# Gated tiles turned between projections, attention's inputs read by 256 tokens with the bias in two parts, memory low parts on two engines

## The chip, the cores and the metric

One core of one Trainium2 chip. The time is the device time of one launch in microseconds. Engines are named as in the profile: PE (TensorE matmuls), PEld (its weight loads), DVE (VectorE), ACT (ScalarE), POOL (GpSimd), SP (SyncE, which only issues transfers here).

## The reference, cut to what matters

Sequence and width are 1024. `@` products are held in float32 quality. Cut to the parts that the change touches:

```
h = layer_norm(x)
proj = h @ w_in                                   # 1024 x 2560
z_a, q_b, k_b, v_b = split(proj)                  # 1024, 512, 512, 512 columns
u, v = split(gelu(z_a)); v = layer_norm(v)        # 512 columns each
s = w_sp(masked, 4 groups of 128x128) @ v + b_sp  # within blocks of 128 tokens
y_a = u * s
# attention: 8 heads of 64; a chunk of 64 queries sees its chunk and 8 before it
scores = q_b k_b^T / 8 + rel_bias[clip(distance, -128, 128)]
y_b = softmax(scores) @ v_b
h = layer_norm(a*h + [y_a, y_b] @ w_out)
k, v = mem @ w_xk, mem @ w_xv                     # memory: 256 x 1024
h = layer_norm(a*h + cross_attention(h @ w_xq, k, v) @ w_xo)
h = layer_norm(a*h + peer(h))                     # expert retrieval, untouched
```

## The kernel before, in words

Every float32 operand of a product is split in two fp32r parts, a high one (ACT, `Copy`) and a low one (raw minus high, on DVE or POOL), and `three` (L106 to L108) issues three matmuls per product. The stages run one after the other, with a barrier and freed semaphores (`free_sems`) between them. Each stage is written out per engine; an engine runs its instructions in order and waits on semaphores. The input of a product is held turned (features on the partitions) in `aT_hi` and `aT_lo`, in an early half (tokens 0 to 511) and a late half.

**Projection** (`project_stage("pin", ..., gated=True)`). 40 units: 5 blocks of 512 columns by 8. Blocks 0 and 1 (units 0 to 15) give u and v through a gelu on ACT; blocks 2 and 3 (16 to 31) give q and k turned; block 4 (32 to 39) gives v_b. A unit is 24 matmuls of 512 columns on PE, one copy out of PSUM (ACT for gelu, DVE at L620 else) and one store by SP (L565). In block 4 unit 32 + i reads token tile i of `aT`. While a block runs, the four weight pieces of the next are loaded by SP at even units (L549), their high parts are made by ACT (L584), the low parts of pieces 0 and 2 by POOL (L574), those of 1 and 3 by DVE (L608, at units 2 and 6 of a block).

**Gating** (`class Gating`) rides on these units. `tile(u, delay)` says which of the 8 token tiles has a step at unit u: tile j loads at unit 16 + 3j (L410, L413), is normalised by DVE at 17 + 3j (`vector_step`, L444 to L453), and is mixed by PE at 19 + 3j (12 matmuls of 128 columns before the unit's own), with y = (s + b) u on DVE (L461) in the same step. With EVERY = 3 tile 7 is mixed at step 40, behind the last unit. Then `finish_tensor`, `finish_scalar` and `finish_vector` turn the eight y tiles: 4 transposes on PE (L496), a high part (L502) and a low part (L507) each, over two PSUM banks, into the first four feature groups of `aT`.

**Attention** (`attention_stage`). 64 units: 8 query tiles of 128 tokens by 8 heads. Tile n looks at nk = 128, 256, 384, 512 keys for n = 0 to 3 and at 640 from n = 4 on. Per unit PE makes scores (three or six matmuls), DVE adds the bias and takes the maximum (L789) and its negative (L793), ACT takes the exponential (L761), DVE the reciprocal (L800) and the product (L802), PE turns the probabilities (L839), ACT and DVE split them (L755, L808), PE multiplies by v. Step u has the scores and softmax of unit u, the product of u - 1, the turning of u - 2 and the values of u - 3; the outputs of a pair of heads are split every second step (L769, L813). The inputs come back from HBM in 12 pieces of 512 KB through a raw buffer of two places: q and k by 128 features of all 1024 tokens (rows of 4 KB), in turn for the four pairs of heads, then v by 256 tokens. SP waits for a piece's low part before it loads the next but one. Pieces 2u + 2 and 2u + 3 are split in step u (ACT L744; DVE L775 for q and k, POOL L738 for v), behind the softmax of unit u. The bias, 640 columns of 8 heads spread over 128 partitions (2,560 KB), is one transfer behind the first two pieces (L726); POOL masks two corners of it (L733, L734), and DVE's first L789 waits for both.

**Memory** (`memory_stage`). Four blocks of 512 columns of `w_xk` and `w_xv`, each in four weight pieces over four raw places: SP loads (L901) when the low part of the piece four before is made, ACT makes the high part (L924), POOL every low part (L908). PE runs 4 units of 24 matmuls of 256 columns for each block of w_xk, and 2 of 24 of 512 columns for each of w_xv.

Behind this come the projection of w_xq, cross attention, a norm stage, the key scores and the expert stages, which take the rest of the span from about 660 us on.

Of the kernel before, what the change touches and what calls it, by code (L numbers as in the profile page):

```python
# [57 lines left out]
def layer_program(nc, x, mem, ln_in_g, ln_in_b, w_in, gate_ln_g, gate_ln_b, w_sp, b_sp, rel_bias, w_out,  # L58
# [51 lines left out]
    with top:  # L110
# [247 lines left out]
        class Gating:  # L358
# [3 lines left out]
            FIRST, EVERY, SETUP = 16, 3, 8  # L362
# [127 lines left out]
            def finish_tensor(self, pe):  # L490
                for j in range(TT):
# [7 lines left out]
            def finish_scalar(self, act):  # L499
                for j in range(TT):  # L500
# [3 lines left out]
            def finish_vector(self, dve):  # L504
                for j in range(TT):
# [4 lines left out]
        def project_stage(tag, weight, blocks, gated=False):  # L510
# [21 lines left out]
            with ExitStack() as stage:  # L532
# [7 lines left out]
                after = range(len(units), len(units) + 3)  # L540
                with nc.Block() as block:
# [36 lines left out]
                    def _(act):  # L578
# [9 lines left out]
                        for u, (b, i) in enumerate(units):  # L588
# [7 lines left out]
                            if gated:  # L596
                                gate.scalar_step(act, u)
                        if gated:
                            for u in after:
                                gate.scalar_step(act, u)  # L600
                            gate.finish_scalar(act)

                    @block.vector
                    def _(dve):
# [8 lines left out]
                        for u, (b, i) in enumerate(units):  # L613
# [7 lines left out]
                            if gated:  # L621
                                gate.vector_step(dve, u)
                        if gated:
                            for u in after:
                                gate.vector_step(dve, u)
                            gate.finish_vector(dve)

                    @block.tensor
                    def _(pe):
                        for u, (b, i) in enumerate(units):  # L630
                            if gated:
                                gate.tensor_step(pe, u)
                            if u >= BANKS:
# [14 lines left out]
                        if gated:  # L648
                            for u in after:
                                gate.tensor_step(pe, u)  # L650
                            gate.finish_tensor(pe)


        def attention_stage():


            bias_in, masked = sem("at_bias_in"), sem("at_masked")
            raw_in = [sem(f"at_raw_in{i}") for i in range(2)]
# [21 lines left out]
            with ExitStack() as stage:  # L680
# [12 lines left out]

                pieces = []
# [19 lines left out]
                with nc.Block() as block:  # L714
                    @block.sync
                    def _(sp):
                        for n, (src, _, _) in enumerate(pieces):

                            if n >= QK + 2:
                                sp.wait_ge(sp_lo_v, n - QK - 1)  # L720
                            elif n >= 2:
                                sp.wait_ge(sp_lo, n - 1)
                            sp.dma_start(raw_of(n), src).then_inc(raw_in[n % 2], 16)
                            if n == 1:

                                sp.dma_start(bias[:], bass.AP(ext_d.tensor, ext_d.offset,  # L726
                                                              [[1, P], [EXT, B_HEADS], [1, SPAN]])).then_inc(bias_in, 16)

                    @block.gpsimd
                    def _(pool):  # L730

                        pool.wait_ge(bias_in, 16)
# [3 lines left out]
                        for n in range(QK, len(pieces)):  # L736
# [1402 lines left out]
```

## Time and profile before

| | us |
|---|---|
| median of 3 runs | 3589.03 (3585.22 to 3593.11) |
| the profiled execution, its own time | 3612.53 |
| its span | 3610.7 |
| PE busy | 3108.0 (86%) |
| DVE busy | 2120.6 (59%) |
| POOL busy | 1449.8 (40%) |
| mean granted clock | 0.931 |

The span is that of one profiled execution, whose own time stands 23.5 us above the median of the runs; durations below are from it. A stretch gives its length, then for PE, PEld, DVE, ACT and POOL the busy time with the number of instructions, then PEclk, the busy share of the DMA engines and their GB/s. PEclk is the granted TensorE clock as a share of 2.4 GHz (0.50 is the lower level, 1.2 GHz). In a timeline each row gives start, length, engine, line, operation, tile written and tiles read, and in brackets the idle time before it and what ended it; "x8" are merged instructions. A matmul's length holds its way through the pipeline; the distance of two starts is what it costs.

### The profile page before, as it was taken

How to read it: one execution, taken by the hardware profiler on the slowest of the kernel's cores; microseconds unless marked ns; L12 is line 12 of the kernel's file. 1: busy time of each engine (PE TensorE's matmuls, PEld its weight loads, DVE VectorE, ACT ScalarE, POOL GpSimd, SP SyncE). 2: the span in 40 equal slices, each digit the busy share in tenths (PEclk: the TensorE clock that was granted, in tenths of full speed). 3: DMA queues.
4: the chain of work that ended last, by engine and by line, in shares of the span. 5: the costliest groups of instructions: out<-in, count | busy, mean ns of one | idle time of the engine just before them, and what ended most of it. 6: DMA issues, size and time to landing. Idle time of an engine off the chain costs nothing. (4 is left out here: it accounts for less than half of the span.)

```text
span 3610.7 us, 42790 instructions
## 1 busy us (share of the span) xinstructions
PE 3108.0 (86%) x16184; PEld 2408.3 (67%) x16184; DVE 2120.6 (59%) x4483; ACT 1191.5 (33%) x1931; POOL 1449.8 (40%) x1116
## 2 busy tenths in 40 slices
PE   4995989788879979999999989766659989899997
PEld 3874777677668858888777766544436666676665
DVE  4143784215332267888877686666557667664447
ACT  3212452314221124444333333678712222222222
POOL 3100002410210025555776667667735444524542
PEclk9997599899989989999999999988879999999998
DMA  4333003321323178888999999899999999999993
GB/s 157 105 100 131 1 5 136 117 85 56 130 81 81 49 249 305 329 321 339 391 410 379 410 387 412 309 408 383 393 363 362 351 361 363 353 331 358 389 368 125
DMA packets 368045, 937.45 MB, mean 260 GB/s; under 512 B 31440, under 2 KB 130264, under 8 KB 366816
## 3 DMA queue, kind: packets, MB, share of 16 engines
q0 software_dynamic: 147456, 536.94, 38.8%
q1 hardware_dynamic: 220384, 397.77, 31.0%
q8 instruction: 130, 2.13, 0.2%
q14 instruction: 75, 0.61, 0.0%
HBM read 827.60 MB, written 106.98 MB: 259 GB/s over the span
## 5 line engine op out<-in xcount | busy, mean ns | idle before, releaser
L1419 POOL DMA_INDIRECT ex_ring<-in_expert_v,ex_idxT_sb x400 | 452.6, 1131 | 420.9 <-PE ex_ps_v L1444 217.3
L1419 POOL DMA_INDIRECT ex_ring<-in_expert_u,ex_idx_sb x328 | 407.6, 1243 | 398.7 <-DVE ex_hg L1428 230.6
L1428 DVE CUSTOM_DVE_ANT_0 ex_ring<-ex_ring,ex_xg 128x1024 f32<-128x1024 f32 x328 | 392.7, 1220 | 105.9 <-DMA ex_ring<-in_expert_u,ex_idx_sb 62.7
L106 PE MATMUL eo_ps<-eo_v_hi_sb,aT_late_hi 128*128 128x512 f32 x1024 | 413.2, 404 | 36.6 <-DVE aT_late_lo L2016 36.6
L106 PE MATMUL ex_ps_h<-aT_late_hi,ex_uT_hi_sb 128*128 128x512 f32 x1024 | 414.3, 405 | 34.8 <-issue 17.1
L107 PE MATMUL eo_ps<-eo_v_lo_sb,aT_late_hi 128*128 128x512 f32 x1024 | 404.7, 395 | 0.0
L108 PE MATMUL ex_ps_h<-aT_late_hi,ex_uT_lo_sb 128*128 128x512 f32 x1024 | 403.4, 394 | 0.0
L108 PE MATMUL eo_ps<-eo_v_hi_sb,aT_late_lo 128*128 128x512 f32 x1024 | 402.5, 393 | 0.0
L107 PE MATMUL ex_ps_h<-aT_late_lo,ex_uT_hi_sb 128*128 128x512 f32 x1024 | 401.6, 392 | 0.0
L1444 PE MATMUL ex_ps_v<-ex_ring,ex_w_sb 128*32 128x512 f32 x1600 | 252.8, 669 | 123.8 <-DMA ex_ring<-in_expert_v,ex_idxT_sb 94.3
L2024 DVE TENSOR_TENSOR eo_acc<-eo_acc,eo_ps 128x1024 f32<-128x1024 f32 x124 | 151.3, 1220 | 299.0 <-PE eo_ps L108 222.3
L106 PEld LDWEIGHTS eo_ps<-eo_v_hi_sb,aT_late_hi 128*128 128x128 f32 x1024 | 195.4, 191 | 138.3 <-issue 59.6
L1980 ACT ACTIVATE eo_v_hi_sb<-eo_v_raw 128x1024 fp32r<-128x1024 f32 x124 | 131.3, 1059 | 437.0 <-DMA eo_v_raw<-in_expert_v 336.7
L106 PEld LDWEIGHTS ex_ps_h<-aT_late_hi,ex_uT_hi_sb 128*128 128x128 f32 x1024 | 194.0, 189 | 108.9 <-issue 57.9
L1419 POOL DMA_INDIRECT ex_ring_more<-in_expert_u,ex_idx_sb x161 | 214.8, 1334 | 103.3 <-issue 41.5
L1560 ACT ACTIVATE ex_uT_lo_sb<-ex_ps_t 128x1024 fp32r<-128x1024 f32 x128 | 131.7, 1029 | 376.3 <-PE ex_ps_t L1743 248.9
L1428 DVE CUSTOM_DVE_ANT_0 ex_ring_more<-ex_ring_more,ex_xg 128x1024 f32<-128x1024 f32 x161 | 192.0, 1220 | 57.0 <-DMA ex_ring_more<-in_expert_u,ex_idx_sb 45.7
L108 PEld LDWEIGHTS eo_ps<-eo_v_hi_sb,aT_late_lo 128*128 128x128 f32 x1024 | 195.4, 191 | 42.6
L108 PEld LDWEIGHTS ex_ps_h<-aT_late_hi,ex_uT_lo_sb 128*128 128x128 f32 x1024 | 193.9, 189 | 43.0
L107 PEld LDWEIGHTS eo_ps<-eo_v_lo_sb,aT_late_hi 128*128 128x128 f32 x1024 | 195.7, 191 | 38.8
L107 PEld LDWEIGHTS ex_ps_h<-aT_late_lo,ex_uT_hi_sb 128*128 128x128 f32 x1024 | 194.4, 190 | 36.9
L1444 PEld LDWEIGHTS ex_ps_v<-ex_ring,ex_w_sb 128*32 128x32 f32 x1600 | 53.5, 116 | 234.8 <-issue 234.0
(332 smaller groups left out, 6629.4 us busy)
## 6 DMA issues: line engine op xcount, KB each, us to landing
ex_u_raw<-in_expert_u SPq DMA_DIRECT2D x128, 512.0 KB
eo_v_raw<-in_expert_v SPq DMA_DIRECT2D x124, 512.0 KB
act_d<-ex_act SPq DMA_DIRECT2D x128, 256.0 KB
gate_d<-ex_gate SPq DMA_DIRECT2D x8, 4096.0 KB
eo_g_raw<-gate_d SPq DMA_DIRECT2D x64, 512.0 KB
eo_a_raw<-act_d SPq DMA_DIRECT2D x124, 256.0 KB
h_d<-n_row SPq DMA_DIRECT2D x24, 512.0 KB, 2.6
pin_raw<-in_w_in SPq DMA_DIRECT2D x20, 512.0 KB
```

The costliest lines, as they stand in the source:

```text
L106: pe.matmul(ps, l_hi, r_hi, start=first, stop=False)
L107: pe.matmul(ps, l_hi, r_lo, start=False, stop=False)
L108: return pe.matmul(ps, l_lo, r_hi, start=False, stop=last)
L1419: pool.indirect_dma_start(rows(n), None, table, bass.IndirectOffsetOnAxis(at, 0)).then_inc(ring_in[slot[n]], 16)
L1428: dve.tensor_tensor_reduce(out=u, in0=u, in1=xg[:, j, :], scale=1.0, scalar=0.0, op0=ALU.mult, op1=ALU.add, accum_out=hg[:, j, k:k + 1]).t ...
L1444: last = pe.matmul(ps_v[32 * q:32 * q + 32, col], spreads[:, q, 31 * i + 31:31 * i + 63], rows(at[q])[:, col], start=i == 0, stop=i == 31)
L1560: act.activation(uT_lo[:, e % 2, :, :], ps_t[e % 2][:].rearrange("p (k t) -> p k t", t=P), ACT.Copy).then_inc(uT_lo_done, 1)
L1980: act.activation(v_hi[:, b, x, :], v_raw(e), ACT.Copy).then_inc(v_hi_done, 1)
L2024: dve.tensor_tensor(acc[:, t, :], acc[:, t, :], ps[t % 2][:], ALU.add).then_inc(added[t % 2], 1)
```

## The change

In gating EVERY becomes 2, so that tile j loads at unit 16 + 2j, is normalised at 17 + 2j and mixed at 19 + 2j (tile 7 at unit 33), and tile j is turned at step 34 + j: six of them before units 34 to 39, two behind the last. In attention q, k and v are read by 256 tokens (q and k with rows of 1 KB over all four feature groups), all q and k pieces without a wait, since their raw data lies in the room of the v parts of the same tokens; the bias is read in a near part (128 columns of each head, rows of 512 bytes) and a far part (512 columns). The pieces of tokens 256 and up are split in named later steps (`SPLIT_AT`), and the first low and high parts needed are those of tile pair 0 alone. The first softmax waits for the near mask, that of tile 1 for the far one. In the memory stage DVE makes every odd low part.

```diff
-            FIRST, EVERY, SETUP = 16, 3, 8
+            FIRST, EVERY, SETUP, TURN = 16, 2, 8, 34
...
-            def finish_tensor(self, pe):
-                for j in range(TT):
+            def turned(self, u):
+                return u - self.TURN if 0 <= u - self.TURN < TT else None
+
+            def turn_tensor(self, pe, u):
+                j = self.turned(u)
+                if j is not None:
                     pe.wait_ge(self.y_done, A_GROUPS * (j + 1))
                     if j >= 2:
                         pe.wait_ge(self.lo_done, j - 1)
...
-                after = range(len(units), len(units) + 3)
+                after = range(len(units), Gating.TURN + TT)
...
                             if gated:
                                 gate.scalar_step(act, u)
+                                gate.turn_scalar(act, u)
                         if gated:
                             for u in after:
-                                gate.scalar_step(act, u)
-                            gate.finish_scalar(act)
+                                gate.turn_scalar(act, u)
...
                             if gated:
                                 gate.vector_step(dve, u)
+                                gate.turn_vector(dve, u)
...
                             if gated:
                                 gate.tensor_step(pe, u)
+                                gate.turn_tensor(pe, u)
                             if u >= BANKS:
                                 out_of_psum(pe, u - BANKS)
...
-                for f in range(QF):
-                    pieces.append((qb_d[f * P:(f + 1) * P, :], q_hi[:, f, :], q_lo[:, f, :]))
-                    pieces.append((kb_d[f * P:(f + 1) * P, :], k_hi[:, f, :], k_lo[:, f, :]))
                 for f in range(TT // 2):
-                    pieces.append((vb_d[2 * f * P:2 * (f + 1) * P, :].rearrange("(a p) n -> p a n", p=P),
+                    tok = slice(f * W, (f + 1) * W)
+                    for d, hi, lo in ((qb_d, q_hi, q_lo), (kb_d, k_hi, k_lo)):
+                        pieces.append((d[:, tok].rearrange("(f p) t -> p f t", p=P), hi[:, :, tok], lo[:, :, tok]))
+                    pieces.append((vb_d[f * W:(f + 1) * W, :].rearrange("(a p) n -> p a n", p=P),
                                    v_hi[:, 2 * f:2 * f + 2, :], v_lo[:, 2 * f:2 * f + 2, :]))
-                QK = 2 * QF
+                SPLIT_AT = {0: (2,), 2: (3,), 3: (4,), 5: (5,), 10: (6,), 11: (7,), 13: (8,), 18: (9,), 19: (10,), 21: (11,)}
 
                 def raw_of(n):
-                    r = raw[:, n % 2, :]
-                    return r if n < QK else r.rearrange("p (a n) -> p a n", a=2)
+                    f, part = divmod(n, 3)
+                    if part == 2:
+                        return raw[:, f % 2, :].rearrange("p (a n) -> p a n", a=2)
+                    return (v_hi, v_lo)[part][:, 2 * f:2 * f + 2, :].rearrange("p a n -> p (a n)").bitcast(F32).rearrange("p (f t) -> p f t", f=QF)
...
+                        load(0)
+                        load(1)
+                        sp.dma_start(bias[:, :, 0:P], spread_bias(0, P)).then_inc(near_in, 16)
+                        for n in range(2, 6):
+                            load(n)
+                        sp.dma_start(bias[:, :, P:SPAN], spread_bias(P, SPAN)).then_inc(far_in, 16)
+                        for n in (6, 7, 9, 10):
+                            load(n)
+                        for f in range(2, TT // 2):
+                            sp.wait_ge(sp_lo_v, f - 1)
+                            load(3 * f + 2)
...
+                        pool.wait_ge(near_in, 16)
                         pool.memset(bias[0:CHUNK, :, 0:CHUNK], MASKED).then_inc(masked, 1)
+                        pool.wait_ge(masked, 1)
+                        split_v(0)
+                        pool.wait_ge(far_in, 16)
+                        pool.wait_ge(sp_lo_v, 1)
                         pool.memset(bias[CHUNK:P, :, SPAN - CHUNK:SPAN], MASKED).then_inc(masked, 1)
...
-                            for n in range(2 * u + 2, min(2 * u + 4, len(pieces))):
+                            for n in SPLIT_AT.get(u, ()):
                                 split(n)
...
-                            if n == 0 and hd % 2 == 0:
-                                pe.wait_ge(sp_lo, 2 * (hd // 2) + 2)
+                            if n % 2 == 0 and hd == 0:
+                                pe.wait_ge(sp_lo, n + 2)
...
-                                sp.wait_ge(lo_done, n - 3)
+                                sp.wait_ge(lo_done[n % 2], n // 2 - 1)
...
-                        for n in range(4 * PIECES):
+                        for n in range(0, 4 * PIECES, 2):
...
-                        for u in range(len(units)):
+                        n = 1
+                        for u, (b, i) in enumerate(units):
+                            while n < min(4 * PIECES, (b + 2) * PIECES):
+                                nb, q = divmod(n, PIECES)
+                                dve.wait_ge(hi_done, n + 1)
+                                dve.tensor_tensor(w_lo[:, nb % 2, 2 * q:2 * q + 2, :], raw[:, n % 4, :, :],
+                                                  w_hi[:, nb % 2, 2 * q:2 * q + 2, :], ALU.subtract).then_inc(lo_done[1], 1)
+                                n += 2
                             dve.wait_ge(out_hi, u + 1)
```

## Rows read from the trace of the kernel before

**Rows 1.** The page: granted clock in 40 slices of 90.27 us, in tenths

```profile
PEclk9997599899989989999999999988879999999998
```

**Rows 2.** Stretches of attention (first six) and of the memory stage: length, engines, PEclk, DMA

```profile
319.20:332.10 12.90, 0.91 (x6) 0.72 (x6) 2.46 (x3) 3.40 (x3) 1.04 (x2) 0.50 0.93 357
332.10:367.50 35.40, 10.40 (x42) 8.18 (x42) 15.98 (x54) 16.13 (x36) 9.35 (x4) 0.50 0.37 122
367.50:384.90 17.40, 16.63 (x78) 13.64 (x79) 12.90 (x57) 8.92 (x33) 0.00 (x0) 0.50 0.00 1
384.90:408.30 23.40, 23.40 (x110) 18.65 (x111) 15.85 (x57) 10.27 (x32) 0.00 (x0) 0.50 0.00 1
408.30:436.50 28.20, 28.20 (x145) 21.97 (x146) 18.50 (x57) 12.07 (x32) 0.00 (x0) 0.55 0.00 1
436.50:532.00 95.50, 84.72 (x821) 75.73 (x822) 84.30 (x226) 56.88 (x128) 0.00 (x0) 1.00 0.01 1
658.00:726.00 68.00, 53.24 (x304) 48.05 (x304) 8.43 (x14) 22.84 (x30) 37.71 (x16) 0.84 0.43 139
```

**Rows 3.** Waits of PE, 60 to 330 us: total, times, longest

```profile
PE ga_ps_s L106 <- DVE ga_v_lo L453: 4.6, 8, 2.4
```

**Rows 4.** Timeline of PE, projection: start, length, what, idle before it

```profile
229.31 0.39 PE L108 MATMUL pin_ps<-aT_late_hi,pin_wlo 128*128 128x512 f32 x1
...
232.05 0.33 PE L106 MATMUL ga_ps_s<-ga_v_hi,ga_wT_hi 128*128 128x128 f32 x1 [2.35 <-DVE ga_v_lo L453]
...
234.37 0.73 PE L106 MATMUL pin_ps<-aT_early_hi,pin_whi 128*128 128x512 f32 x1
...
242.16 0.39 PE L106 MATMUL pin_ps<-aT_late_hi,pin_whi 128*128 128x512 f32 x1
...
252.81 0.39 PE L108 MATMUL pin_ps<-aT_early_hi,pin_wlo 128*128 128x512 f32 x1
...
254.80 0.45 PE L106 MATMUL pin_ps<-aT_late_hi,pin_whi 128*128 128x512 f32 x1
```

**Rows 5.** Timeline of all engines, end of projection to the first softmax

```profile
307.72 0.68 DVE L620 TENSOR_SCALAR pin_res<-pin_ps 128x512 f32<-128x512 f32 x1
...
309.25 1.06 PE L496 MATMUL ga_ps_y<-ident,ga_y_sb 128*128 128x128 f32 x8
...
316.94 1.29 DVE L507 TENSOR_TENSOR aT_late_lo<-ga_ps_y,aT_late_hi 128x512 fp32r<-128x512 f32 x2 [0.84 <-ACT aT_late_hi L502]
...
319.15 0.32 SPq L723 DMA_DIRECT2D at_raw<-qb_d  x1
...
323.07 1.06 ACT L744 ACTIVATE at_q_hi<-at_raw 128x1024 fp32r<-128x1024 f32 x1 [5.57 <-DMA at_raw<-qb_d]
...
332.09 0.29 DVE L789 CUSTOM_DVE_ANT_0 at_prob<-at_ps_s,at_bias 128x128 f32<-128x128 f32 x1 [5.46 <-POOL at_bias L734]
```

**Rows 6.** Timeline of DVE in attention: a piece's low part; softmaxes of tile 3

```profile
334.08 1.23 DVE L775 TENSOR_TENSOR at_q_lo<-at_raw,at_q_hi 128x1024 fp32r<-128x1024 f32 x1 [1.51 <-ACT at_q_hi L744]
...
426.40 0.69 DVE L789 CUSTOM_DVE_ANT_0 at_prob<-at_ps_s,at_bias 128x512 f32<-128x512 f32 x1 [0.38 <-PE at_ps_s L108]
430.30 0.69 DVE L789 CUSTOM_DVE_ANT_0 at_prob<-at_ps_s,at_bias 128x512 f32<-128x512 f32 x1 [1.54 <-PE at_ps_s L108]
```

**Rows 7.** Tokens of 512 bytes a row read by cross attention: issue to landing

```profile
DMA to landing us min/median/max: 4.0/4.6/5.4
```

**Rows 8.** Waits of PE, 655 to 730 us

```profile
PE me_ps L106 <- POOL me_wlo L908: 7.5, 4, 5.5
```

**Rows 9.** Memory stage: POOL's timeline, then stretches as in rows 2

```profile
669.22 18.72 POOL L908 TENSOR_TENSOR me_wlo<-me_raw,me_whi 128x1024 fp32r<-128x1024 f32 x8 [16.17 <-ACT me_whi L924]
...
671.70:678.60 6.90, 4.92 (x18) 4.06 (x18) 0.00 (x0) 1.75 (x3) 6.90 (x4) 0.50 0.61 179
678.60:682.80 4.20, 4.20 (x19) 4.20 (x20) 0.00 (x0) 1.70 (x2) 4.20 (x2) 0.50 0.75 225
682.80:690.10 7.30, 7.30 (x63) 7.30 (x62) 1.18 (x3) 1.99 (x4) 5.15 (x3) 0.99 0.74 225
```

More of the change, by code:

```diff
@@ L497, in finish_tensor, with turn_scalar, turn_vector @@
                     last.then_inc(self.tr_done, 1)
-            def finish_scalar(self, act):
-                for j in range(TT):
+            def turn_scalar(self, act, u):
+                j = self.turned(u)
+                if j is not None:
                     act.wait_ge(self.tr_done, j + 1)
                     act.activation(self.part(aT_hi, j), self.bank(j), ACT.Copy).then_inc(self.hi_done, 1)
-            def finish_vector(self, dve):
-                for j in range(TT):
+            def turn_vector(self, dve, u):
+                j = self.turned(u)
+                if j is not None:
                     dve.wait_ge(self.hi_done, j + 1)
@@ L649, in _ @@
                             for u in after:
-                                gate.tensor_step(pe, u)
-                            gate.finish_tensor(pe)
+                                gate.turn_tensor(pe, u)
         def attention_stage():
-            bias_in, masked = sem("at_bias_in"), sem("at_masked")
-            raw_in = [sem(f"at_raw_in{i}") for i in range(2)]
+            near_in, far_in, masked = sem("at_near_in"), sem("at_far_in"), sem("at_masked")
+            raw_in = [sem(f"at_raw_in{i}") for i in range(3 * TT // 2)]
             sp_hi, sp_lo, sp_lo_v = sem("at_split_hi"), sem("at_split_lo"), sem("at_split_lo_v")
@@ L716, in _, with load @@
                     def _(sp):
[L717 to L727, printed above, removed]
+                        def load(n):
+                            sp.dma_start(raw_of(n), pieces[n][0]).then_inc(raw_in[n], 16)
@@ L729, in _, with split_v @@
                     @block.gpsimd
                     def _(pool):
-                        pool.wait_ge(bias_in, 16)
+                        def split_v(f):
+                            n = 3 * f + 2
+                            pool.wait_ge(sp_hi, n + 1)
+                            pool.tensor_tensor(pieces[n][2], raw_of(n), pieces[n][1], ALU.subtract).then_inc(sp_lo_v, 1)
+                        pool.wait_ge(near_in, 16)
                         pool.memset(bias[0:CHUNK, :, 0:CHUNK], MASKED).then_inc(masked, 1)
+                        pool.wait_ge(masked, 1)
@@ L734, in _ @@
+                        split_v(0)
+                        pool.wait_ge(far_in, 16)
+                        pool.wait_ge(sp_lo_v, 1)
                         pool.memset(bias[CHUNK:P, :, SPAN - CHUNK:SPAN], MASKED).then_inc(masked, 1)
                         pool.wait_ge(masked, 2)
-                        for n in range(QK, len(pieces)):
-                            pool.wait_ge(sp_hi, n + 1)
-                            pool.tensor_tensor(pieces[n][2], raw_of(n), pieces[n][1], ALU.subtract).then_inc(sp_lo_v, 1)
+                        for f in range(1, TT // 2):
+                            split_v(f)
@@ L778, in _ @@
                         split(1)
-                        dve.wait_ge(masked, 2)
+                        dve.wait_ge(masked, 1)
                         for u in range(NU + 3):
@@ L783, in _ @@
                                 _, nk, parts = keys(n)
+                                if n == 1 and hd == 0:
+                                    dve.wait_ge(masked, 2)
                                 dve.wait_ge(s_done, u + 1)
@@ L793, in _ @@
                                 dve.tensor_scalar(neg[:, u % 2:u % 2 + 1], top_s[:, u % 2:u % 2 + 1], -1.0, None, ALU.mult).then_inc(neg_done, 1)
-                            for n in range(2 * u + 2, min(2 * u + 4, QK)):
-                                split(n)
+                            for n in SPLIT_AT.get(u, ()):
+                                if n % 3 < 2:
+                                    split(n)
                             if 1 <= u < NU + 1:
@@ L870, in memory_stage @@
             raw_in = [sem(f"me_raw_in{i}") for i in range(4)]
-            hi_done, lo_done, mm_done, out_hi, out_lo = sem("me_hi"), sem("me_lo"), sem("me_mm"), sem("me_out_hi"), sem("me_out_lo")
+            hi_done, mm_done, out_hi, out_lo = sem("me_hi"), sem("me_mm"), sem("me_out_hi"), sem("me_out_lo")
+            lo_done = [sem(f"me_lo{i}") for i in range(2)]
             PIECES = 4
```

14 lines of the change are left out of this document (9 added, 5 removed).

## The prediction

> **What bounds the kernel now.** I read the page first. The chain that ended last lies in the expert stages, which the change does not touch; the edited stages end before the first fifth of the span, each ends with a barrier, and so what one of them saves reaches the end in full if its own last wait moves. The row of the granted clock has one thing to see besides: its two lowest digits, 7 and 5, are the fourth and fifth of 40 slices, 271 to 451 us [rows 1], and the stretches say it sharply [rows 2]: from 319.2 to 408.3 us the clock is 0.50, the lower level (1.2 GHz), and it is 1.00 from 436.5 us on. So I cut attention into its query tiles and asked for the stretches. The reader should see three regimes. Until the first softmax at 332.1 us everything waits for transfers (DMA share 0.93). Tile 0, 35.4 us for eight units of the smallest size, has no busy engine at all (PE 10.40, DVE 15.98, ACT 16.13): it is paced by reading and splitting all of q and k. Tiles 1 to 3 have PE busy 16.63 of 17.4, 23.40 of 23.4 and 28.20 of 28.2 us, at the half clock: PE bounds them. From tile 4 on, at the full clock, DVE with 84.30 and PE with 84.72 of 95.5 us share the bound, 95.5 / 32 = 2.98 us a unit.
>
> For the projection I read PE's waits and its timeline. PE is full there. It waits 8 times, 4.6 us in all, for the normalised gating tile, and half of that is one wait of 2.35 us before 232.05 us [rows 3, 4]. Behind it the matmuls are at the lower clock: twelve of them take from 234.37 to about 239.4 us. The tail behind the last unit runs from 307.7 to 318.2 us (last low part), and attention's first transfer is issued at 319.15 us [rows 5]. In the memory stage PE waits four times, 7.5 us, for POOL, which makes eight low parts without a pause at 2.34 us each [rows 8, 9].
>
> **The sum, part by part.**
>
> *Projection, the tail.* Time from the last unit's end (307.65) to the issue at 319.15 is 11.5 us. After the change the tail holds: DVE's copy of unit 39 (0.68, ends 307.65 + 0.7 in the old clock), the low part of tile 5 (half of 1.29), PE's transposes of tile 7 (1.06 / 8 × 4 = 0.53), which need that low part's bank, then a high part (0.6) and a low part (0.65), and the same 0.9 to the issue: 0.7 + 0.65 + 0.6 + 0.6 + 0.7 + 0.9 = 4.15 us with hand-overs. Tile 6 lies beside that. The tail gives −7.35. The last store is out by then too: it needs DVE's copy and some 2 us, which ends before the last low part.
>
> *Projection, what moves in.* PE pays inside for what it paid outside: one more mixing and six turnings. A mixing costs 254.80 − 252.81 less one matmul's 0.23 = 1.76 us in the stream, its 0.21 wait included [rows 4]. A turning is four transposes at 0.13 plus a change of operand, 0.6: in all 1.76 + 6 × 0.6 = +5.4 us. ACT's and DVE's share of a turning (0.6 and 0.65) lies beside PE's 5.5 us unit; if that cover were gone, PE would wait for a bank at the next turning but one.
>
> *Projection, the one stall.* At unit 26 DVE has both a weight piece's low part (units 18, 22, 26, 30) and a normalisation (17 + 3j). With EVERY = 2 normalisations fall on odd units only, so the two never meet. The stall's price is 242.16 − 229.31 = 12.85 us against 1.99 + 5.51 = 7.50 for an undisturbed mixing and unit (the next one): −5.35, of which 2.1 is the wait and 3.2 the lower clock [rows 4]. A second wait of 0.9 (unit 22), within the 4.6 of [rows 3], loses 0.7. In their place DVE does a normalisation and y in one odd step, 0.7 + 5.0 + 1.1 = 6.8 us; y comes behind the normalisation, so PE's 0.21 stays, and the even step behind it (1.23 + 0.7) ends within two units (11 us). SP, too, is held in every even step by the wait for y before it loads u, and its store and next weight load go 1 to 2 us later; the copy of unit u waits for the store four units before, so nobody waits. Projection: −7.35 + 5.4 − 5.35 − 0.7 = **−8.0**. Bounds: −2 (the stall returns at another unit), −10.
>
> *Attention to the first softmax.* Before: issue at 319.15, high part of q from 323.07, of k, low parts, scores done at about 327.6; then DVE stands 5.46 us for the masks, and the first softmax is at 332.09, 12.9 us after the issue [rows 5]. The bias had 2.6 MB behind 1 MB of q and k, at 357 GB/s [rows 2]. Now the near part is 0.5 MB, and 1.5 MB land in about 4.5 + 2 us. The rows of q and k shrink from 4 KB to 1 KB; rows of 512 bytes land in 4.0 to 5.4 us for 512 KB [rows 7], against the 3.9 of the 4 KB ones, so I add at most 0.7. The first softmax then waits for the low part of k, not for the mask: 8.4 to 9.5 us after the issue, **−4.2**.
>
> *Tile 0.* All q and k pieces were split there, at 1.06 and 1.23 us [rows 5, 6]. Now six of the eight remain in the loop behind the first two, in steps 2, 3, 10, 11, 18, 19. A step with such a piece is a chain: softmax 0.5, exponential 0.6, high part 1.06, low part 1.23, reciprocal, product and low part of the probabilities 0.7, with hand-overs 4.6 us; DVE does nothing else meanwhile. A plain step lies between DVE's work and the PE-bound pace of tile 1: 12.90 / 8 = 1.6 and 17.4 / 8 = 2.2; I take 1.9. Tile 0: 2 × 4.6 + 6 × 1.9 = 20.6 us against 35.4: **−14.8**. The far bias (5.5 MB in the queue by its end, 16 to 20 us after the issue at the rate of rows 2) and its mask are there before tile 1 begins at 29.
>
> *Tiles 1 and 2.* They get two split steps each: 5.0 us in place of 2.2 and of 2.9, so +5.6 and +4.2. PE has its next scores done when DVE comes back, and the step behind runs at DVE's pace and not at PE's, which recovers about 0.7 of each: **+7.0**. The v pieces cost ACT 1.06 at steps 5, 13, 21, in slack (ACT 10.27 of 23.4): **+0.4** in all.
>
> *The clock in tile 3.* Before, it came back in the last unit of that tile (mean 0.55 there) [rows 2]; steady units are 3.90 us apart at the lower level [rows 6] and 2.98 at the upper one with even more keys. Where in the tile it comes back is not in the source, and the order of matmuls per unit is unchanged; I take the middle of the tile: 4 × 0.9 = **−3.6**. Attention: −4.2 − 14.8 + 7.0 + 0.4 − 3.6 = −15.2.
>
> *Memory.* PE starts at the same time, with the first low part (POOL, 669.22 + 2.34). DVE makes piece 1 in 1.23 meanwhile, so three waits of 0.65 go, and PE is dense from 671.7 us and not from 678.6. The clock came back at about 682.8, 4.2 us after that; at the lower level a matmul costs 4.2 / 20 = 0.21 us, at the upper 7.3 / 63 = 0.12 [rows 9]. If it comes back 4.2 us into the dense stream again: 20 matmuls low, 76 high, block 0 ends at 671.7 + 4.2 + 9.1 = 685.0 against 690.1, the end of the last of these stretches. **−5.0**; −2 if the clock rises where it did. The pieces of block 1 are loaded as early or earlier; DVE has 8.43 us of work in 68 there [rows 2].
>
> **Sum**: −8.0 − 15.2 − 5.0 = −28. The profiled execution (3612.5, span 3610.7) would come to 3584; the median of the runs is 23.5 us below it, and I take the difference off that: 3589 − 28 = **3561**.
>
> One place where page and trace differ. The row first: PE is busy without a gap at 0.50 for all of tile 2 and nearly all of tile 3, 50 us. The Trainium skill's TensorE: Matmul & The Clock Gate (Part 1) says that activity releases the throttle. This trace contradicts it for attention's small matmuls, and agrees in the memory stage [rows 2, 9]. If the page held here, the clock would be up from tile 1 on; that is the first rival.
>
> **The rivals.**
> 1. *The clock is up early* (0.15). The new start is denser, and what takes PE from 0.50 could come already in tile 1 or 2. Worked from rows: a unit at the full clock is bound by DVE or by 2.98 us, so tile 2 could fall from 23.4 to about 17, tile 3 from 28.2 to 22, against −3.6 counted: −9 to −12 more, 3550. Against it: in tile 2 PE was as dense as it can be and got nothing, and the new split steps put holes of 2 to 3 us there.
> 2. *Slower: the clock stays down into tiles 4 to 7* (0.06). Place: the 32 units of 640 keys. Price: from 2.9 and 3.9 us at 384 and 512 keys the lower level gives about 4.6 for 640, so +1.6 a unit. The gain of 28 is gone after 17 such units; if the clock never came back, 32 × 1.6 = +51 and the time is 3589 − 25 + 51 = 3615. For it: tile 3's rise was late. Against: tile 4 has more matmul work per unit than tile 3, which sufficed.
> 3. *The holes bite* (0.17). Split steps cost more than 5 us, or ACT's v pieces delay the chain, and the projection stalls at another unit: +6 in tiles 1 and 2, +4 in the projection, 3571 to 3578.
> 4. *It does little* (0.08): the pace of tile 0 is kept by something else, as landing of q1, k1 and v0 behind one another in one queue; then −8 − 5 + 7 and little else, 3583.
>
> **How the numbers follow.** The forecast has 0.54. 8 times in 10 the time lies between 3546 (rival 1 whole) and 3582 (rival 3 with a clock that rises a few units into tile 4, 1.6 each). A measurement of this kernel can tell about 0.2% from no change, 7.2 us: faster is below 3581.9. Forecast, rival 1, rival 3 and a part of rival 4 are faster: 0.88. Rival 4's rest and a part of rival 2: 0.06. Slower: 0.06.
>
> **What would show it.** Right: no wait of PE for the gating tile above 1 us and clock 1.00 throughout 160 to 307 us; last unit of the projection at 307, attention's first issue at 311; first softmax 8.4 to 9.5 us behind it; tile 0 in 18 to 22 us, tiles 1 and 2 longer than before by 3 to 4 each; the first memory block 5 us shorter. Wrong: a first softmax that still waits for POOL's mask; a wait of tile 1's first softmax on the far mask; split steps above 6 us; a clock of 0.50 behind the start of tile 4.

## The result, and the profile of the kernel after

| | before | after |
|---|---|---|
| median of 20 runs each | 3594.94 us | 3579.68 us |
| lowest to highest | 3583.86 to 3626.09 | 3555.36 to 3600.51 |
| ratio of after to before, 95% interval | | 0.9949, 0.9928 to 0.997 |
| the profiled execution's own time | 3612.53 | 3577.55 |

The kernel is faster by 0.5%, some 18 us with an interval of 11 to 26 us. The forecast was 28 us and a time of 3561 (range 3546 to 3582). Both kernels spread by 40 us from run to run, so what each step did is read in the traces, stage by stage. The two profiled executions lie 35 us apart, more than the kernels do: 27.6 us of that stand before the expert stages' first PE work, the rest behind it. The page of after, span and granted clock:

```profile
span 3575.8 us, 42797 instructions
...
PEclk9997799898989999999999999888879999999998
```

The low digits stand where they stood [rows 1]: attention's tiles 0 to 2 and a part of tile 3 still run at the lower clock. The next lines have the same stretches of the kernel after as [rows 2]: to the first softmax, tiles 0 to 3, tiles 4 to 7, and the memory stage.

```profile
312.40:320.90 8.50, 0.91 (x6) 0.72 (x6) 2.49 (x3) 3.40 (x3) 0.52 (x1) 0.60 0.88 284
320.90:338.20 17.30, 10.21 (x42) 8.20 (x42) 11.14 (x51) 9.47 (x30) 5.22 (x3) 0.50 1.01 345
338.20:362.20 24.00, 16.74 (x78) 13.65 (x79) 16.82 (x59) 11.70 (x35) 2.36 (x1) 0.50 0.07 23
362.20:390.60 28.40, 23.52 (x110) 18.64 (x111) 18.95 (x59) 13.10 (x35) 2.37 (x1) 0.50 0.00 1
390.60:414.30 23.70, 22.46 (x144) 17.50 (x144) 18.08 (x56) 12.12 (x32) 0.00 (x0) 0.74 0.00 1
414.30:511.00 96.70, 85.58 (x835) 76.65 (x835) 84.36 (x227) 57.53 (x129) 0.00 (x0) 1.00 0.01 1
637.00:701.00 64.00, 50.64 (x304) 45.99 (x304) 28.68 (x22) 22.89 (x30) 22.03 (x8) 0.88 0.44 148
```

Against [rows 2] the wait for the first softmax fell from 12.9 to 8.5 us and tile 0 from 35.4 to 17.3, while tiles 1 and 2 grew from 17.4 to 24.0 and from 23.4 to 28.4 us. In these two PE is no longer full (16.74 of 24.0, 23.52 of 28.4). Tile 3 took 23.7 us in place of 28.2, because the clock came back in its middle here (mean 0.74, before 0.55).

PE's wait for the gating tile, which answers to [rows 3]:

```profile
PE ga_ps_s L106 <- DVE ga_v_lo L453: 1.7, 8, 0.3
```

The wait of 2.35 us is gone, and with it the stretch at the lower clock behind it (the clock was 1.00 in every stretch of 10 us from 160 to 310 us). The end of the projection and attention's start, against [rows 5] (each row: start, length, engine, line, what, idle before):

```profile
307.59 0.39 PE L108 MATMUL pin_ps<-pin_whi,aT_late_lo 128*128 128x512 f32 x1
...
308.02 0.69 DVE L627 TENSOR_SCALAR pin_res<-pin_ps 128x512 f32<-128x512 f32 x1 [4.62 <-PE pin_ps L108]
...
309.45 0.63 PE L501 MATMUL ga_ps_y<-ident,ga_y_sb 128*128 128x128 f32 x4 [1.03 <-DVE aT_late_lo L514]
...
310.75 0.69 DVE L514 TENSOR_TENSOR aT_late_lo<-ga_ps_y,aT_late_hi 128x512 fp32r<-128x512 f32 x1 [0.84 <-ACT aT_late_hi L508]
312.36 0.37 SPq L731 DMA_DIRECT2D at_v_hi<-qb_d  x1
...
315.93 1.06 ACT L769 ACTIVATE at_q_hi<-at_v_hi 128x1024 fp32r<-128x1024 f32 x1 [5.21 <-DMA at_v_hi<-qb_d]
...
318.52 1.23 DVE L800 TENSOR_TENSOR at_k_lo<-at_v_lo,at_k_hi 128x1024 fp32r<-128x1024 f32 x1 [0.28 <-ACT at_k_hi L769]
...
320.86 0.29 DVE L816 CUSTOM_DVE_ANT_0 at_prob<-at_ps_s,at_bias 128x128 f32<-128x128 f32 x1 [1.11 <-PE at_ps_s L108]
```

The last unit's last matmul starts at 307.59 (307.26 before), tile 7 is turned behind the low part of tile 5, and attention's first transfer is issued at 312.36 instead of 319.15: −6.8 us. The low part of k ends at 319.75, and the first softmax waits for the scores that need it, no longer for POOL's mask.

In tile 0, the softmaxes (L816) and the two low parts (L800) on DVE, and below them what DVE waited for in tiles 0 to 2:

```profile
322.31 0.28 DVE L816 CUSTOM_DVE_ANT_0 at_prob<-at_ps_s,at_bias 128x128 f32<-128x128 f32 x1
...
324.73 1.67 DVE L800 TENSOR_TENSOR at_q_lo<-at_v_hi,at_q_hi 128x1024 fp32r<-128x1024 f32 x1 [1.94 <-ACT at_q_hi L769]
...
326.91 0.28 DVE L816 CUSTOM_DVE_ANT_0 at_prob<-at_ps_s,at_bias 128x128 f32<-128x128 f32 x1
...
329.26 1.23 DVE L800 TENSOR_TENSOR at_k_lo<-at_v_lo,at_k_hi 128x1024 fp32r<-128x1024 f32 x1 [1.87 <-ACT at_k_hi L769]
...
331.00 0.28 DVE L816 CUSTOM_DVE_ANT_0 at_prob<-at_ps_s,at_bias 128x128 f32<-128x128 f32 x1
```

```profile
DVE at_q_lo L800 <- ACT at_q_hi L769: 6.2, 3, 2.2
DVE at_k_lo L800 <- ACT at_k_hi L769: 5.6, 4, 1.9
```

From 322.31 to 326.91 and from there to 331.00 the two steps with a piece take 4.6 and 4.1 us; those of tiles 1 and 2 took 5.3, 4.2, 5.7 and 4.7. DVE stands 11.8 us in all for ACT's high parts, 0.3 us of it before the first softmax.

One more pair of lines from tile 1, first DVE, then POOL:

```profile
356.88 2.27 DVE L830 TENSOR_SCALAR at_prob<-at_prob,at_rinv 128x256 f32<-128x256 f32 x1
```

```profile
356.64 2.36 POOL L750 TENSOR_TENSOR at_v_lo<-at_raw,at_v_hi 128x1024 fp32r<-128x1024 f32 x1 [18.69 <-ACT at_v_hi L769]
```

DVE's product of step 14, the step behind a v piece, takes 2.27 us and ends 0.15 us behind POOL's low part of v. That step takes 3.87 us, against 2.60 in the kernel before; step 22 takes 3.47 against 3.05 in the same way.

The memory stage, the low parts by engine (min/median/max ns), first of after, then of before:

```profile
L937 POOL TENSOR_TENSOR me_wlo<-me_raw,me_whi x8: 2362/2510/3384, 648.5 to 680.5; 128x1024 fp32r<-128x1024 f32 x8
L970 DVE TENSOR_TENSOR me_wlo<-me_raw,me_whi x8: 1626/2592/3418, 649.4 to 681.5; 128x1024 fp32r<-128x1024 f32 x8
```

```profile
L908 POOL TENSOR_TENSOR me_wlo<-me_raw,me_whi x16: 2357/2398/2437, 669.2 to 710.2; 128x1024 fp32r<-128x1024 f32 x16
```

And PE there from the first low part on, with the clock in the column behind POOL:

```profile
650.90:653.40 2.50, 2.37 (x11) 2.40 (x12) 2.50 (x2) 0.38 (x1) 2.50 (x1) 0.50 0.42 138
653.40:655.40 2.00, 1.68 (x8) 1.38 (x8) 1.88 (x1) 0.17 (x1) 0.80 (x1) 0.50 0.89 281
655.40:657.40 2.00, 2.00 (x18) 2.00 (x17) 0.00 (x0) 1.20 (x2) 1.04 (x1) 0.97 0.88 299
657.40:665.00 7.60, 7.60 (x66) 7.60 (x65) 4.30 (x5) 3.80 (x6) 3.98 (x2) 1.00 0.75 237
```

PE runs 11 and 8 matmuls at the lower clock and is at the full one from about 655.4 us, 4.4 us behind its start; before, it was 11 us behind it [rows 9]. From PE's start to the start of DVE's last output took 52.4 us before and takes 48.1 now. PE's waits for a low part, against [rows 8]:

```profile
PE me_ps L106 <- POOL me_wlo L937: 5.8, 2, 5.5
```

The first wait of 5.5 us stands as before, and 0.3 us is left of the other 2.0. There is one thing the forecast did not have: DVE's subtraction takes 2.59 us by the median and not 1.23, when POOL's runs beside it. PE shows no wait for DVE's low parts.

### The profile page after: what moved, and what is told of

Same layout as the page of the kernel before. It is cut to its first block and busy times, and to the rows that moved or that the text cites. A ratio compares the mean times of both kernels' runs of the same rounds, so it can differ in the third digit from the quotient of the medians.

```text
span 3575.8 us, 42797 instructions
## 1 busy us (share of the span) xinstructions
PE 3100.9 (87%) x16184; PEld 2402.6 (67%) x16184; DVE 2144.1 (60%) x4491; ACT 1189.6 (33%) x1931; POOL 1451.7 (41%) x1108
## 5 line engine op out<-in xcount | busy, mean ns | idle before, releaser
L1455 POOL DMA_INDIRECT ex_ring<-in_expert_u,ex_idx_sb x328 | 416.6, 1270 | 408.0 <-DVE ex_hg L1464 218.7
```

The source lines that it names most:

```text
L1455: pool.indirect_dma_start(rows(n), None, table, bass.IndirectOffsetOnAxis(at, 0)).then_inc(ring_in[slot[n]], 16)
```

## The experiments

All ratios are against runs of the kernel before on the same chip. The granted clock and the late stages differ from run to run, and so the verdict of each experiment rests on the length of its stage in its trace. e7, e8 and e11 were run once each and have no ratio.

**Each part alone, and all again.** The kernel before with one of the three parts, and the changed kernel once more:

```diff
# e1: class Gating and project_stage as changed, the rest as before
# e2: attention_stage as changed, the rest as before
# e3: memory_stage as changed, the rest as before
# e4: the changed kernel
```

> Only the gating part of the change on the kernel before. Theory A (each part's saving passes to the end): attention's first transfer is issued 6.5 to 7.5 us earlier than the 319.15 of before, no wait for the gating tile above 0.4 us, clock 1.00 throughout the projection, attention itself unchanged in its first tile (35.4 us), total 6 to 8 us less. Theory B (a part of what is saved early is given back in the late stages, which wait for transfers): the same at attention's start, but the total only 0 to 4 us less.

> Only the attention part on the kernel before. Theory A: first softmax 8.5 us behind the first issue (before 12.9), tile 0 17.3 us, tiles 1 and 2 about 24 and 28 us, tile 3 between 20 and 28 us according to where the clock comes back; attention 12 to 19 us shorter, and the total as much less. Theory B: the total only 5 to 10 us less.

> Only the memory part on the kernel before. Theory A: PE starts block 0 with the first low part as before and its stream from there to the last unit is 48 us instead of 52.4, 4 to 5 us less, total 4 to 5 less. Rival: the clock comes back where it did and only the waits go, 2 us. Theory B: total unchanged.

> The changed kernel as it is, beside the three parts on the same chip. If the parts add up (theory A), its total is less than before by the sum of the three, 23 to 30 us, and by the trace the stages up to the key scores are 24 to 26 us shorter. Theory B: less than the sum. In tile 3 of attention the clock comes back at another unit than in the first profile if its place is chance, at the fourth or fifth again if the order of the work fixes it.

| | ratio (95% interval) | first issue of attention | tiles 0, 1, 2 | tile 3 | tile 4 | memory | from the expert stages' first PE work to the end |
|---|---|---|---|---|---|---|---|
| before | | 319.15 | 35.4, 17.4, 23.3 | 28.2 | 23.2 | 52.4 | 2336 |
| after | 0.9949 (0.9928 to 0.997) | 312.36 | 17.3, 24.1, 28.3 | 23.8 | 23.5 | 48.1 | 2329 |
| e1 | 0.9963 (0.9939 to 0.9987) | 311.84 | 35.4, 17.4, 23.3 | 30.1 | 23.6 | 52.4 | 2298 |
| e2 | 0.9957 (0.9928 to 0.9986) | 318.84 | 17.4, 24.1, 28.3 | 27.6 | 23.4 | 52.1 | 2315 |
| e3 | 0.9974 (0.9947 to 1.0002) | 319.60 | 35.5, 17.4, 23.3 | 26.3 | 23.5 | 47.9 | 2311 |
| e4 | 0.9954 (0.9929 to 0.9979) | 312.42 | 17.3, 24.1, 28.4 | 30.2 | 26.9 | 48.0 | 2312 |

Each part does alone what it does in the whole, to 0.1 us in tiles 0 to 2. Gating gives 7.3 us (6.7 to 6.8 with the rest), memory 4.5. The first issue moves a little from run to run where the projection is the same: it stands at 318.84 to 319.60 in the three kernels with gating as before, and at 310.55 to 312.42 in the nine with gating as changed (all runs but before, e2, e3 and e11), so by the means gating gives 7.8 us. In e2, whose projection is as before, PE's wait for the gating tile is back:

```profile
PE ga_ps_s L106 <- DVE ga_v_lo L453: 4.4, 8, 2.2
```

Tile 3 is the exception. The same kernel took 23.8 us there in one run and 30.2 in another, and in the latter it went on into tile 4. Two stretches of e4, tile 3 and tile 4:

```profile
390.60:420.80 30.20, 30.20 (x145) 23.68 (x146) 18.63 (x57) 12.07 (x32) 0.00 (x0) 0.50 0.00 1
420.80:447.70 26.90, 25.93 (x197) 23.29 (x197) 20.87 (x57) 13.82 (x32) 0.00 (x0) 0.77 0.01 2
```

At 0.50 the whole tile is PE's (30.20 of 30.20), its units take 3.4 to 4.2 us and tile 4's first units 4.2; in after the clock was back after three and a half units. So the place of the clock's return differs between two runs of one kernel, and tiles 3 and 4 together were 9.8 us longer in e4 for it.

e4 thus missed what was expected of it: its total was 16.7 us below before by the medians, not 23 to 30, and the expert stages' first PE work came 17.7 us earlier, not 24 to 26 (27.6 in after; 4.3, 12.0 and 7.4 in e1, e2 and e3). Tiles 3 and 4, where the clock comes back, account for it. With their length taken out, that point comes 23.5 us earlier than before in after, 23.4 in e4, and 24.2 in e1, e2 and e3 added up. So up to there the parts add, as theory A has it. The totals by themselves don't show it: the ratios of e1, e2 and e3 add up to 1.06% and e4 has 0.46%, each with an interval of 0.2 to 0.3% to either side. Theory B was about the stages behind that point. They took between 2298 and 2336 us with no order in what the kernel was, e1 the least and before the most: no sign of a give-back, but one of a few us would be lost in that spread and stays open.

**The split step.** e5 makes the low part one step behind the high part, e6 makes it on POOL:

```diff
# e5, vector engine
-                            for n in SPLIT_AT.get(u, ()):
+                            for n in SPLIT_AT.get(u - 1, ()):
                                 if n % 3 < 2:
                                     split(n)
# e6: these three lines go; on GpSimd, before split_v(f) of f = 1 to 3
+                            for n in (3 * f, 3 * f + 1):
+                                pool.wait_ge(sp_hi, n + 1)
+                                pool.tensor_tensor(pieces[n][2], raw_of(n), pieces[n][1], ALU.subtract).then_inc(sp_lo_p, 1)
...
# ACT and PE wait for sp_lo_p in place of sp_lo from the second tile pair on
```

> The changed kernel with DVE making the low part of a q or k piece in the step behind the one in which ACT makes the high part, so that DVE no longer stands idle for ACT's exponential and high part. Theory (a split step is a chain of exponential, high part and low part, about 3 us over a plain step, of which only 1.2 is DVE's own work): each of the six split steps falls from about 5.2 to about 3.5 us, tile 0 from 17.3 to about 14, tiles 1 and 2 from 24.1 and 28.3 to about 21 and 26 us. Rival (the time is DVE's and ACT's work itself, or the landing of the pieces): the tiles keep their lengths within 1 us.

> The changed kernel with the low parts of all q and k pieces behind the first two on POOL (2.35 us each there) in place of DVE. Theory of the chain: split steps cost only ACT's 1.06 us, tile 0 about 14 us, tile 1 about 19, tile 2 about 24.5, 10 us less in all than the changed kernel, if DVE's own instructions keep their length beside POOL. Rival: DVE's instructions beside POOL's get up to twice as long and take back half of it; or PE waits at the start of tile 2 for POOL, which stands behind the far mask.

The tiles 0 to 3 of e5:

```profile
319.60:334.00 14.40, 10.26 (x42) 8.21 (x42) 12.18 (x51) 9.59 (x30) 5.22 (x3) 0.50 1.08 370
334.00:355.00 21.00, 16.71 (x78) 13.63 (x79) 16.58 (x59) 11.70 (x35) 2.36 (x1) 0.50 0.18 62
355.00:379.80 24.80, 23.46 (x110) 18.63 (x111) 18.74 (x59) 13.22 (x35) 2.36 (x1) 0.50 0.00 1
379.80:404.10 24.30, 23.04 (x144) 17.83 (x144) 18.07 (x56) 12.11 (x32) 0.00 (x0) 0.72 0.00 1
```

14.4, 21.1 and 24.7 us in place of 17.3, 24.1 and 28.3: 9.5 us shorter, 1.6 for each of the six steps, with the same instructions on every engine (DVE busy 12.18, 16.58 and 18.74 us, in after 11.14, 16.82 and 18.95). DVE has no wait for ACT's high parts left in these tiles (11.8 us in after). The theory of the chain holds, and the time of a split step was in its waits. The totals: 0.9895 of before (0.9848 to 0.9941, 3541.81 us median), and in a second series, named e10, 0.9944 (0.9918 to 0.9971) with tiles of 14.2, 21.0 and 24.7.

> The kernel of e5 once more, to set it against the changed kernel's 0.995: 0.990 to 0.993 of before, tiles 0, 1 and 2 of attention again 14.4, 21.1 and 24.7 us, tile 3 anything from 21 to 30 us. The rival, that e5's 0.9895 was the noise of the late stages, gives 0.995.

e10's ratio missed the expected 0.990 to 0.993 and is the rival's 0.995 within its interval, so the low 0.9895 of e5, from four runs, was in part noise, and the totals alone don't show e5 to be better than after. The traces do, by 9.5 us, twice. Both series beat the kernel before.

e6 took 20.0, 21.2 and 24.4 us in tiles 0 to 2 (0.9907, 0.9884 to 0.9929). It was expected to be 10 us shorter than after in these tiles and was 4 us shorter. Tiles 1 and 2 are as in e5, and not the expected 19 in tile 1: four of DVE's products (L833) took 1.61 to 2.36 us in the two tiles, beside POOL's instructions and to their end, where after has two such, as the rival had it. Tile 0 holds one long step, in which ACT waited:

```profile
ACT at_v_hi L775 <- POOL at_k_lo L764: 6.3, 1, 6.3
```

POOL stood before the far mask until 330.39 us, its low parts of q and k came behind it, and ACT's next v piece needed the room of the raw data: the queue of one engine had become the bound. Moving the work was worth no more than moving it one step.

**The bias in one part.**

```diff
-                        sp.dma_start(bias[:, :, 0:P], spread_bias(0, P)).then_inc(near_in, 16)
+                        sp.dma_start(bias[:], spread_bias(0, SPAN)).then_inc(near_in, 16)
...
-                        sp.dma_start(bias[:, :, P:SPAN], spread_bias(P, SPAN)).then_inc(far_in, 16)
```

> The changed kernel with the bias read in one part (2,560 KB) behind the first two pieces, everything else as changed. Theory: the first softmax waits for the mask again, 12.5 to 13 us behind the first issue in place of 8.5; tile 0 as long as with two parts or up to 2 us longer, since q, k and v of the second pair stand behind the bias in the queue. Rival: the earlier first softmax is only the small pieces' doing and stays below 10 us.

```profile
324.14 0.52 POOL L752 MEMSET at_bias<- 64x512 f32 x1 [82.26 <-DMA at_bias<-ext_d]
324.69 0.29 DVE L814 CUSTOM_DVE_ANT_0 at_prob<-at_ps_s,at_bias 128x128 f32<-128x128 f32 x1 [5.95 <-POOL at_bias L752]
```

The first issue was at 311.34, so the first softmax came 13.35 us behind it, 4.9 later than with two parts, and it waited for POOL's mask. Tile 0 took 17.3 us, as after. So the 4.4 us gained before the first softmax are the bias's, and tile 0's 18 us are not; what is left of the change there is the pieces by 256 tokens with their later steps, which need no split of all q and k at once.

**Turning behind the last unit.**

```diff
-            FIRST, EVERY, SETUP, TURN = 16, 2, 8, 34
+            FIRST, EVERY, SETUP, TURN = 16, 2, 8, 40
```

> The changed kernel with all eight gated tiles turned behind the last unit as before, gating still every 2 units. Theory (the tail saves about 7 us and six turnings in the stream cost 3 to 4): the last unit ends at about 304, the tail to attention's first issue is about 10 us, that issue comes 3 to 4 us later than the changed kernel's 312.4. Rival: turning between the units costs as much as it saves, and the issue comes at the same time.

The last matmul started at 304.0 (307.6 in after: six turnings cost 0.57 us each after 0.2 us of a later start is taken off) and attention's first issue was at 314.06, 1.7 us later than after. The theory had 3 to 4: the tail was 5.3 us longer, the stream 3.4 us shorter. Against the mean issue of the nine runs with gating as changed, 311.4, it is 2.6 us. Their last matmuls start at 305.8 to 307.7, so one run of e11 says only that a turning costs 0.3 to 0.6 us. Most of gating's gain is thus not the turning but the closer steps: 5.1 of 6.8 us are there without it.

**The clock.** e8 gives PE matmuls of no use while it waits and behind the scores of units 0 to 30; e9 gives e5 one burst of twelve behind unit 20's scores:

```diff
+                        def filler(count):
+                            for _ in range(count):
+                                pe.matmul(ps_s[1][:, HALF:D], aT_hi[0][:, 0, 0:P], aT_hi[0][:, 1, :], start=True, stop=True)
+                        filler(30)                       # e8
                         for u in range(NU + 3):
                             if u < NU:
                                 scores(u)
+                            if u < 31:                   # e8; in e9: if u == 20: filler(12)
+                                filler(2)
```

> The changed kernel with matmuls of no use (128x128 by 512, into a free bank, outputs unchanged): 30 on PE while it waits for the first pieces, then two behind the scores of each of the first 31 units. Theory (the clock stays at 1.2 GHz through tiles 0 to 3 because attention's start leaves PE idle for about 9 us and its small matmuls bring it back only by chance): the granted clock stays 1.00 or comes back in tile 0 or 1; tile 3 takes about 21 us and tile 2 about 25 in place of 24 to 30 and 28. Rival: the clock falls in tile 0 all the same, and the fillers at 1.2 GHz cost up to 0.8 us a unit where PE is the bound, tiles 2 and 3 up to 6 us longer each.

> The kernel of e5 with 12 matmuls of no use (128x128 by 512 into a free bank) behind the scores of unit 20, outputs unchanged. Theory (in tiles 2 and 3 PE's own small matmuls bring the clock back only by chance, dense large ones bring it back at once, as in the memory stage): the burst costs 4 to 6 us, the clock is 1.00 from tile 2's second half on, tile 3 takes 21 us in every run in place of 24 to 30; attention as long as or up to 3 us shorter than e5's, and the same from run to run. Rival: the clock falls again in tile 3, since its matmuls do not hold it; then the burst only costs 5 us.

e8, stretches of 10 us from 310 us on:

```profile
310.00:320.00 10.00, 8.98 (x33) 7.06 (x33) 2.52 (x3) 3.41 (x3) 0.52 (x1) 0.83 0.79 253
320.00:330.00 10.00, 5.97 (x29) 3.65 (x28) 5.02 (x20) 5.04 (x13) 2.38 (x1) 0.92 1.07 378
330.00:340.00 10.00, 8.96 (x34) 7.10 (x34) 7.92 (x32) 4.55 (x17) 2.88 (x2) 0.50 0.72 224
340.00:350.00 10.00, 9.51 (x32) 6.65 (x30) 4.78 (x19) 4.20 (x14) 0.00 (x0) 0.50 0.10 40
```

The clock had fallen at about 311.3 us, behind a gap of 2.31 us in PE's work. The thirty dense fillers brought it back at about 314.7, and it stayed full to about 328.4, 1.5 us behind the end of a gap of 2.50 us in which PE stood behind a split step. Then it stayed down, though PE was busy for 8.96 of 10 us. From there the fillers cost: tiles 0 to 2 took 20.1, 27.6 and 30.8 us, 8.8 more than after. Only tile 3 was at its best, 21.1. e9, the burst, what came behind it, the hole and the rest:

```profile
366.00:370.00 4.00, 4.00 (x13) 3.05 (x13) 2.54 (x7) 0.00 (x0) 0.00 (x0) 0.59 0.00 0
370.00:376.00 6.00, 4.91 (x46) 4.05 (x44) 4.38 (x14) 4.61 (x12) 0.88 (x1) 1.00 0.01 3
376.00:378.00 2.00, 0.31 (x2) 0.00 (x0) 2.00 (x2) 0.56 (x4) 1.49 (x1) 0.52 0.02 4
378.00:406.00 28.00, 27.63 (x138) 21.17 (x139) 18.15 (x57) 11.74 (x32) 0.00 (x0) 0.55 0.00 1
```

```profile
374.49 0.52 PE L867 MATMUL at_ps_t<-ident,at_prob 128*128 128x128 f32 x3 [1.09 <-DVE at_pT_lo L836]
378.31 0.88 PE L867 MATMUL at_ps_t<-ident,at_prob 128*128 128x128 f32 x3 [2.00 <-DVE at_pT_lo L836]
```

The clock was 0.59 in the stretch of the burst and 1.00 in the one behind it. A mean of 0.52 from 376 to 378 us puts the fall at about 376.1, while PE was still at work; the hole of 2.00 us begins 0.2 us later, so it is not what brought the clock down. The longest gap between the rise and the fall is the 1.09 us before 374.49. The hole itself is DVE's: its product of 128x384 ran from 375.11 for 2.59 us (0.42 in the next step) beside POOL's low part of v, of 375.12 to 377.48. Tile 2 took 27.4 instead of 24.7 us, tile 3 26.9, as in e10 without the burst; the total was 0.9954 (0.9926 to 0.9982). Both rivals won in what they said of the clock, at smaller prices: dense large matmuls bring it up, and in attention's first tiles it falls again. In both runs and in the projection before (gap to 232.05 [rows 4], fall at about 232.4) the fall comes 0.3 to 1.6 us behind the end of a gap of 1.09 to 2.50 us in PE's work; from tile 4 on, gaps of up to 0.83 us in after left it at 1.00. What neither run shows is why it stays down where PE has no gap, as in tiles 2 and 3 of the kernel before.

## Why the prediction was right, and what was off

- *Projection*: forecast −8.0, measured −6.8 (e1: −7.3, by the means of all runs −7.8). The tail took 4.4 us (forecast 4.15), a turning 0.57 us (forecast 0.6; 0.3 to 0.6 by all runs), and the stall at unit 26 went. The rest is that this run started its projection 0.4 us later.
- *First softmax*: −4.2 forecast, −4.4 measured; e7 shows its cause. A row of 1 KB instead of 4 KB cost nothing that can be seen: the first piece of q was split 3.57 us behind the issue, before 3.92.
- *Tile 0*: −14.8 forecast, −18.1 measured. Split steps took 4.6 and 4.1 us as said (4.6), plain steps 1.4 and not 1.9: without PE as a bound they ran at DVE's pace.
- *Tiles 1 and 2*: +7.4 forecast, +11.6 measured. The chain was right (5.3, 4.2, 5.7 and 4.7 us for 5.0; 9.7 us over the same steps before, forecast 9.8). Two terms failed. The larger is the 0.7 us that each step was to recover behind the hole, 2.8 in all: the steps behind the split ones came out 0.5 us longer. PE, at the lower clock, had nothing saved up: its idle time in tile 2, 4.9 us, is what the tile grew by. The other is the v pieces, put at +0.4 in ACT's slack: they cost 1.7 us, in steps 14 and 22, where DVE's product was held beside POOL's low part.
- *The clock in tile 3*: −3.6 forecast. In the profiled pair tile 3 was 4.4 us shorter, and that is luck: the place of the return moves from run to run in both kernels. Tiles 3 and 4 together took 51.4, 53.8 and 49.8 us with attention as before (before, e1, e3), and 47.3, 51.1, 57.1, 48.5 and 47.3 as changed (after, e2, e4, e7, e11), means of 51.7 and 50.3 with a spread of 10. The step that failed is to read one run's place as the kernel's and to count the way to the tile's middle as a gain: the means give 1.4 us, within the spread.
- *Memory*: −5.0 forecast, −4.3 measured, by the waits and by the earlier clock, both as said.

Without the clock the measured terms are −6.8 − 4.4 − 18.1 + 11.6 − 4.3 = −22.0, which lies in the interval of the ratio (−11 to −26); with 28 I was outside it. The sum was 2.6 us too large in its other terms, and that is a difference of larger errors: tile 0 gave 3.3 us more than forecast and tiles 1 and 2 took 4.2 more. The clock's 3.6 is no gain of the kernel that the profiles can show. The time of 3561 was also set from a median of three runs of before, 3589, that came out at 3595 in twenty; with 3595 the same sum gives 3567. Rival 1 (the clock is up early) did not happen in any run of the changed kernel. The Trainium skill's page TensorE: Matmul & The Clock Gate, Part 1, says that activity releases the throttle. Large dense matmuls did so in the memory stage and in e9; attention's small ones, dense for 30.2 us in e4, had not yet done so, and why is open. Rival 2 (slower) showed its first step in e4, where the lower clock reached four units into tile 4 and took 3.4 us. Rival 3 is true of the holes' cost but they cost 4 us more, not 6, and the projection did not stall. Rival 4 is refuted by tile 0.

## What to carry to other kernels

When one engine makes the first half of a piece of work and another the second, try the second half a step later in the program: here the same instructions took 1.6 us less for each of six pieces. Work that is spread over a loop costs the wait of its chain and not its busy time, so count the wait where the loop has no slack. Where the clock's return moves from run to run, read it in several traces before it stands in a sum, and judge a change of 0.5% by the lengths of its stages as well, as the late stages' spread of 38 us covers it in any single run.

## What the runs showed of the hardware that was not expected

A DVE instruction that reads and writes only on-chip buffers can be held by POOL's beside it. In e5 the product of 128 columns (L830) took 1.96 us in one step and 0.28 in the next, and the long one ended with POOL's low part; first DVE, then POOL:

```profile
322.38 1.96 DVE L830 TENSOR_SCALAR at_prob<-at_prob,at_rinv 128x128 f32<-128x128 f32 x1
...
326.17 0.28 DVE L830 TENSOR_SCALAR at_prob<-at_prob,at_rinv 128x128 f32<-128x128 f32 x1
```

```profile
321.91 2.35 POOL L750 TENSOR_TENSOR at_v_lo<-at_raw,at_v_hi 128x1024 fp32r<-128x1024 f32 x1 [2.35 <-ACT at_v_hi L769]
```

The same was seen of the product in step 14 of after (2.27 us, above) and of the one of 128x384 in e9:

```profile
375.11 2.59 DVE L830 TENSOR_SCALAR at_prob<-at_prob,at_rinv 128x384 f32<-128x384 f32 x1
```

In each case it ended 0.1 to 0.2 us behind POOL's instruction. In the memory stage the same was seen of the subtraction (1.63 to 3.42 us against 1.23), while POOL's own grew from 2.40 to 2.51 by the median. DVE's other instructions between 335.6 and 337.7 us of after, which read PSUM or a single column, kept their lengths beside POOL's.

And the granted clock fell in e9 at about 376.1 us with no gap in PE's work above 1.09 us since its rise, while it stayed down through 30 us of PE busy without a gap in e4.
